# One tile and one product for k and q of the gated delta heads, q without its meta columns, and a new list of places for the steps of the mix

## What is computed

```python
h = concatenate([meta, x])                          # 272 tokens
p = rms_norm(h) @ w_in                              # k, v, q, z of the delta branch; q, k, v of the other (fox)
q, k, v = silu(causal_conv(p_q, p_k, p_v))          # 4 taps
q, k = l2_normalize(q) * DK ** -0.5, l2_normalize(k)
a_mat = strict(k_beta @ k.T * decay)                # k by k
w_val, w_key = triangular_solve(a_mat + I, ...)
qk_intra = causal(q @ k.T * decay)                  # k by q
o, S = scan over chunks of (qk_intra, q * exp(g), k, w_val, w_key)
h = h + (sigmoid(gate_a) * (y_a @ w_o_gdn) + sigmoid(gate_b) * (y_b @ w_o_fox)) @ w_out
```

## Time and profile before

| | |
|---|---|
| median of 3 runs | 2969.7 us (2968.08 to 2970.41) |
| profiled execution | 2970.13 us, its span 2968.4 us |
| TensorE busy | 2916.4 us, 98% of the span |
| DVE, ACT busy | 1926.5 us (65%), 1450.7 us (49%) |
| mean granted TensorE clock | 0.989 |
| DMA | 159 GB/s over the span |

### The profile page before, as it was taken

How to read it: one execution, slowest core, us unless ns; L and a number is a source line. 1 busy time by engine, 2 the same in 40 slices (tenths; PEclk the granted TensorE clock), 3 DMA queues, 4 the chain that set the end, 5 groups by cost and what they waited for, 6 DMA issues and landing times.

```text
span 2968.4 us, 56482 instructions
## 1 busy us (share of the span) xinstructions
PE 2916.4 (98%) x20507; PEld 2677.9 (90%) x20507; DVE 1926.5 (65%) x3349; ACT 1450.7 (49%) x2515; POOL 277.0 (9%) x229
## 2 busy tenths in 40 slices
PE   7999999999999999999999999999999999999998
PEld 7999999999999799998888888888899998999987
DVE  6667776777677454445775665656776666767766
ACT  5555655565556444444444443444545444445543
POOL 0000000000000000001550000000450002400014
PEclk9999999999999899999999999999999999999999
DMA  5434343434343255555555555555554444543344
GB/s 192 143 120 141 120 147 120 138 123 144 122 134 127 93 184 184 188 179 196 181 184 190 183 191 177 190 192 183 190 181 168 143 160 145 179 163 132 133 138 173
DMA packets 128959, 472.94 MB, mean 159 GB/s; under 512 B 14368, under 2 KB 14368, under 8 KB 128672
## 3 DMA queue, kind: packets, MB, share of 16 engines
q1 hardware_dynamic: 126144, 459.46, 46.1%
q0 software_dynamic: 2656, 11.33, 1.2%
HBM read 468.50 MB, written 2.24 MB: 159 GB/s over the span
## 4 chain that ended last, share of the span: by engine, by line
PE 94%; POOL 2%; issue 2%; DVE 1%; ACT 1%; DMA 1%; POOLq 0%; DVEq 0%; ACTq 0%
PE bank L286 20%; PE bank L288 17%; PE bank L289 16%; PE bank L290 16%; PE bank L287 10%; PE bank L725 1%; PE bank L797 1%; PE bank L776 1%; PE bank L958 1%; PE bank L793 1%; POOL late_sum L432 1%; POOL late_sq L428 1%; PE bank L952 1%; PE bank L1030 1%; PE bank L1029 1%
## 5 line engine op out<-in xcount | busy, mean ns | idle before, releaser
L262 DVE TENSOR_TENSOR w_lo<-raw,w_hi 128x1024 fp32r<-128x1024 f32 x866 | 1063.0, 1253 | 249.7 <-ACT w_hi L256 240.5
L256 ACT ACTIVATE w_hi<-raw 128x1024 fp32r<-128x1024 f32 x866 | 898.1, 1053 | 419.5 <-PE bank L287 339.6
L288 PE MATMUL bank<-u,w_hi 128*128 128x256 f32 (+1 forms) x3328 | 1007.8, 303 | 11.7 <-DVE w_lo L262 6.8
L289 PE MATMUL bank<-u,w_hi 128*128 128x256 f32 (+1 forms) x3328 | 950.1, 285 | 0.0
L290 PE MATMUL bank<-u,w_lo 128*128 128x256 f32 (+1 forms) x3328 | 948.4, 285 | 0.0
L288 PEld LDWEIGHTS bank<-u,w_hi 128*128 128x128 f32 x3328 | 631.1, 190 | 36.5 <-issue 22.1
L289 PEld LDWEIGHTS bank<-u,w_hi 128*128 128x128 f32 x3328 | 630.5, 189 | 3.7
L290 PEld LDWEIGHTS bank<-u,w_lo 128*128 128x128 f32 x3328 | 630.2, 189 | 0.0
L286 PE MATMUL bank<-ya,w_hi 128*128 128x512 f32 x1536 | 541.8, 398 | 0.0
L287 PE MATMUL bank<-ya,w_lo 128*128 128x256 f32 x1536 | 430.5, 280 | 0.0
L286 PE MATMUL bank<-u,w_hi 128*128 128x512 f32 x1024 | 359.4, 395 | 0.0
(11 more groups left out here) (365 smaller groups left out, 3757.4 us busy)
## 6 DMA issues: line engine op xcount, KB each, us to landing
raw<-in_stream SPq DMA_DIRECT2D x868, 512.0 KB, 3.4
mix_row<-rows POOLq DMA_DIRECT2D x16, 408.0 KB, 3.9
xT<-in_xT SPq DMA_DIRECT2D x4, 544.0 KB, 6.1
h<-in_xT POOLq DMA_DIRECT2D x1, 2048.0 KB, 9.6
out_dram<-h SPq DMA_DIRECT2D x4, 512.0 KB, 2.6
consts<-in_consts POOLq DMA_DIRECT2D x1, 1921.0 KB, 9.4
vecs<-in_vecs POOLq DMA_DIRECT2D x1, 166.5 KB, 7.0
consts<-in_consts POOLq DMA_DIRECT2D x1, 137.0 KB, 5.9
```

Source lines behind the costliest of these rows:

```text
L256: act.activation(w_hi[:, slot], raw[:, slot], ACT.Copy).then_inc(hi_ready, 1)
L262: dve.tensor_tensor(w_lo[:, slot], raw[:, slot], w_hi[:, slot].bitcast(F32), ALU.subtract).then_inc(lo_ready, 1)
L288: pe.matmul(o, a, x[:, 0], start=first, stop=False)
L289: pe.matmul(o, a, x[:, 1], start=False, stop=False)
```

## The change

- k and q share a tile `kq` of two halves. One product per chunk, with k's chunk as weights and both halves as 256 columns, gives k by k and k by q side by side in bank 6. The meta part of k by k stays in bank 5. The step `qk` of TensorE is gone; `kk` now waits for `unit q` too, and for bank 6 (`gdn y` of the head before). `b mat` and DVE's `qk` read bank 6; `b mat` has one small instruction more.
- q's projection has 260 columns instead of 272 (four meta columns stay for the taps), and conv, tanh, silu, square, sum, root and unit of q have 256 instead of 272.
- The three lists have new places and, in part, another order.

```diff
+Q_FROM = META - 4
+        def u_q(k):
+            return u[:, k, :, Q_FROM:]
-        kT, vT, qT = (mt(x, [P, TOK]) for x in ("kT", "vT", "qT"))
+        kq, vT = mt("kq", [P, 2, TOK]), mt("vT", [P, TOK])
+        kT, qT = kq[:, 0], kq[:, 1]
         PE_PLAN = (
-            (28, "columns"), (76, "k sum"), (81, "turn"), (87, "kk"), (94, "q sum"), (98, "transpose"), (100, "qk"),
-            (105, "prod", 1), (106, "fq sum"), (109, "step", 1), (110, "fk sum"), (111, "prod", 2), (118, "logits"),
-            (120, "step", 2), (120, "turn v"), (120, "prod", 3), (123, "step", 3), (123, "turn p"), (123, "prod", 4),
-            (125, "step", 4), (128, "fox out"), (128, "prod", 5), (131, "meta v"), (132, "step", 5), (135, "prod", 6),
-            (140, "meta state"), (141, "step", 6), (143, "k state", 0), (147, "v new", 0), (152, "state", 0),
-            (167, "k state", 1), (169, "v new", 1), (171, "state", 1), (179, "o sum"))
+            (30, "columns"), (77, "k sum"), (82, "turn"), (85, "q sum"), (93, "kk"), (98, "fq sum"),
+            (100, "transpose"), (106, "prod", 1), (109, "step", 1), (109, "fk sum"), (113, "prod", 2),
+            (117, "logits"), (119, "step", 2), (119, "turn v"), (119, "prod", 3), (122, "step", 3), (122, "turn p"),
+            (122, "prod", 4), (124, "step", 4), (126, "prod", 5), (130, "fox out"), (133, "meta v"), (134, "step", 5),
+            (138, "prod", 6), (140, "meta state"), (141, "step", 6), (143, "k state", 0), (149, "v new", 0),
+            (155, "state", 0), (160, "k state", 1), (164, "v new", 1), (168, "state", 1), (179, "o sum"))
         ACT_PLAN = (
-            (29, "columns"), (56, "tanh", "v"), (64, "tanh", "q"), (65, "tanh", "k"), (67, "tanh", "z"),
-            (69, "k square"), (69, "k root"), (78, "cols"), (80, "decay"), (82, "q square"), (87, "turned"),
-            (93, "q root"), (101, "fq square"), (105, "fq root"), (105, "fk square"), (111, "fk root"), (114, "soft"),
-            (126, "f v"), (127, "f pt"), (127, "f out"), (140, "v new m"), (142, "state"), (152, "v new", 0),
-            (169, "v new", 1), (175, "o square"), (179, "o root"), (182, "y hi"))
+            (25, "columns"), (57, "tanh", "v"), (64, "tanh", "q"), (65, "tanh", "k"), (67, "tanh", "z"),
+            (69, "k square"), (69, "k root"), (80, "q square"), (80, "cols"), (87, "decay"), (87, "q root"),
+            (91, "fq square"), (93, "turned"), (104, "fq root"), (109, "fk square"), (109, "fk root"), (113, "soft"),
+            (125, "f v"), (126, "f pt"), (126, "f out"), (139, "v new m"), (139, "state"), (151, "v new", 0),
+            (169, "v new", 1), (175, "o square"), (179, "o root"), (184, "y hi"))
         DVE_PLAN = (
-            (40, "conv", "v"), (49, "conv", "q"), (54, "silu", "v"), (59, "conv", "k"), (62, "silu", "q"),
-            (63, "silu", "k"), (70, "unit k"), (72, "g diff"), (72, "fox bias"), (78, "silu", "z"), (85, "decay b"),
-            (86, "b mat"), (90, "unit q"), (92, "qk"), (94, "q dec"), (96, "level", 0), (98, "mask", 1),
-            (110, "unit fq"), (111, "level", 1), (111, "unit fk"), (113, "mask", 2), (114, "logits"),
-            (114, "level", 2), (118, "mask", 3), (120, "soft"), (121, "level", 3), (123, "mask", 4),
-            (127, "level", 4), (127, "f out"), (127, "mask", 5), (128, "level", 5), (129, "final"), (135, "mask", 6),
-            (137, "level", 6), (146, "rhs", 0), (156, "state"), (167, "rhs", 1), (180, "y"), (182, "y lo"))
+            (50, "conv", "v"), (55, "conv", "q"), (55, "silu", "v"), (60, "conv", "k"), (61, "silu", "q"),
+            (63, "silu", "k"), (70, "unit k"), (72, "g diff"), (72, "fox bias"), (79, "silu", "z"), (82, "decay b"),
+            (85, "unit q"), (89, "qk"), (94, "b mat"), (94, "level", 0), (95, "q dec"), (97, "mask", 1),
+            (107, "level", 1), (109, "unit fq"), (110, "unit fk"), (111, "mask", 2), (113, "logits"),
+            (113, "level", 2), (116, "soft"), (119, "mask", 3), (123, "level", 3), (123, "mask", 4),
+            (126, "level", 4), (126, "f out"), (126, "mask", 5), (126, "level", 5), (128, "final"), (128, "mask", 6),
+            (133, "level", 6), (148, "rhs", 0), (159, "state"), (163, "rhs", 1), (179, "y"), (189, "y lo"))
             def pe_kk(n):
                 pe.wait_ge(sem("unit k"), n)
+                pe.wait_ge(sem("unit q"), n)
                 if n > 1:
                     pe.wait_ge(sem("prod"), 6 * (n - 1))
-                for t0, w in MAIN_FIRST:
-                    mm = pe.matmul(bank[5][0:w, t0:t0 + w], kT[:, t0:t0 + w], kT[:, t0:t0 + w], start=True,
-                                   stop=True)
-                mm.then_inc(sem("kk"), 1)
+                    pe.wait_ge(sem("gdn y"), 2 * (n - 1))
+                for c, (t0, w) in enumerate(MAIN):
+                    pe.matmul(bank[6][:, c * SEQ:(c + 1) * SEQ].rearrange("p (s n) -> p s n", s=2), kT[:, t0:t0 + w],
+                              kq[:, :, t0:t0 + w], start=True, stop=True)
+                pe.matmul(bank[5][0:META, 0:META], kT[:, 0:META], kT[:, 0:META], start=True,
+                          stop=True).then_inc(sem("kk"), 1)
-            def pe_qk(n):
...
+                    if j == ORDER["q"]:
+                        x, w = u_q, TOK - Q_FROM
...
-                dve.tensor_tensor(b_mat[:], bank[5][:, 0:FOLD], decay_b[:], ALU.mult).then_inc(sem("b mat"), 1)
-                dve.scalar_tensor_tensor(out=prod[:, META:], in0=bank[5][:, FOLD:TOK], scalar=col[:, 2, 0:1],
+                dve.tensor_tensor(b_mat[:, META:], bank[6][:, 0:P], decay_b[:, META:], ALU.mult).then_inc(sem("b mat"), 1)
+                dve.tensor_tensor(b_mat[:, 0:META], bank[5][:, 0:META], decay_b[:, 0:META], ALU.mult).then_inc(
+                    sem("b mat"), 1)
+                dve.scalar_tensor_tensor(out=prod[:, META:], in0=bank[6][:, SEQ:SEQ + P], scalar=col[:, 2, 0:1],
                                          in1=decay_t[:], op0=ALU.mult, op1=ALU.mult).then_inc(sem("b mat"), 1)
```

More of the change, by code:

```diff
@@ L750, in pe_turn @@
                 mm.then_inc(sem("v turned"), 1)
-            def pe_qk(n):
-                pe.wait_ge(sem("unit q"), n)
-                if n > 1:
-                    pe.wait_ge(sem("gdn y"), 2 * (n - 1))
-                for t0, w in MAIN:
-                    mm = pe.matmul(bank[6][0:w, t0:t0 + w], kT[:, t0:t0 + w], qT[:, t0:t0 + w], start=True,
-                                   stop=True)
-                mm.then_inc(sem("qk"), 1)
             def pe_transpose(n):
@@ L894, in _ @@
             steps_pe = {"k sum": lambda n: ones_sum("gdn k", n, TOK), "kk": pe_kk, "turn": pe_turn, "columns": pe_columns,
-                        "q sum": lambda n: ones_sum("gdn q", n, TOK), "qk": pe_qk, "transpose": pe_transpose,
+                        "q sum": lambda n: ones_sum("gdn q", n, SEQ), "transpose": pe_transpose,
                         "fq sum": lambda n: ones_sum("fox q", n, SEQ), "fk sum": lambda n: ones_sum("fox k", n, TOK),
@@ L1187, in act_tanh @@
                     y = {"v": vT, "q": qT, "k": kT}[x]
-                    act.activation(gate_th[:], y[:], ACT.Tanh, scale=0.5).then_inc(sem("silu tanh"), 1)
+                    first = META if x == "q" else 0
+                    act.activation(gate_th[:, first:], y[:, first:], ACT.Tanh, scale=0.5).then_inc(sem("silu tanh"), 1)
             def act_k_square(n):
@@ L1198, in act_q_square @@
                 act.wait_ge(sem("length rs"), norm_of_head("gdn k", n))
-                square("gdn q", n, qT[:], TOK, 0.5)
+                square("gdn q", n, qT[:, META:], SEQ, 0.5)
             def act_fq_square(n):
@@ L1241, in act_decay @@
                     act.wait_ge(sem("decay beta"), n - 1)
-                    act.wait_ge(sem("b mat"), 4 * (n - 1))
+                    act.wait_ge(sem("b mat"), 5 * (n - 1))
                 for c, (t0, w) in enumerate(CHUNKS):
@@ L1313, in _ @@
                          "q square": act_q_square,
-                         "q root": lambda n: root("gdn q", n, TOK, 1.0, ("unit k", n)),
+                         "q root": lambda n: root("gdn q", n, SEQ, 1.0, ("unit k", n)),
                          "turned": act_turned, "fq square": act_fq_square,
@@ L1325, in _ @@
                          "fq": ("fox s", 1), "fk": ("fox s", 1), "fv": ("fox v turned", 1)}
-            dest = {"k": conv_in[0][:, 3:], "v": conv_in[1][:, 3:], "q": conv_in[2][:, 3:], "z": z_raw[:],
+            dest = {"k": conv_in[0][:, 3:], "v": conv_in[1][:, 3:], "q": conv_in[2][:, 3 + Q_FROM:], "z": z_raw[:],
                     "fq": fq[:], "fk": fk[:], "fv": fv[:]}
@@ L1632, in dve_conv @@
                     elif x == "q":
-                        dve.wait_ge(sem("qk"), n - 1)
+                        dve.wait_ge(sem("kk"), n - 1)
                     else:
                         dve.wait_ge(sem("k state"), 2 * (n - 1))
+                first = META if x == "q" else 0
                 for tap in (3, 2, 1, 0):
```

(19 more changed lines are left out.)

6 lines of the change are left out of this document (3 added, 3 removed).

## The result

The changed kernel takes 2978.66 us (median of 9 executions, 2976.56 to 2980.07); the kernel before took 2969.7 beside it (9 executions, 2967.84 to 2973.97). The ratio is 1.0028 with a 95% interval of [1.0019, 1.0038]: slower by 0.28%. The interval excludes no change, and all but its lower end lies beyond 0.2%. 2979.3 us were forecast.

The account below looks back on a forecast made before the run. TensorE was taken as the bound, the mix's time being the sum of its instructions. Savings -4.7, kk's wait +9.8, k sum's wait +3.0 and 17th window +1.5 gave +9.6 us on 2969.7: 2979.3 us, range 2966 to 2987.

Parts of the forecast that it names:

- kk's wait: On TensorE at kk, which now needs unit q: a wait of 0.63 us a head, 9.8 us in all.
- Rivals 1 and 2: First: places on time, only columns show, 2966.5 us, chance 0.18. Second: kk waits 0.3 us, k sum none, some 2972, 0.12.
- Rival 3: Late kk makes b mat late for transpose or prod for DVE: 0.6 us more a head, 2989 us, chance 0.12.
- k sum for k square: TensorE's k sum waits for k square, delayed by DVE's moved conv v: 0.2 us a head, 3.0 us in all.
- the `w_lo` after state starts 0.6 later: On DVE, state starts some 0.9 us later, `w_lo` loses its 0.29 wait, so starts 0.6 us later.
- v new for rhs: In the mix, the rhs was to keep its distance within two places; priced at nothing.
- Columns: q's projection on TensorE: 768 matmuls with 12 columns less, about 5 ns each, save 3.9 us.
- q sum: On TensorE, 16 columns less in two fp32 passes a head save 0.4 us in all.
- Merged product: In kk on TensorE: four passes fewer save 28 ns a head, 0.4 us in all.
- Transpose and the others: Transpose stands 7 places behind kk instead of 11, covered by 0.6 us; it and other moved places priced at nothing.
- 17th window: The window without blocks: soft ahead of mask 3, prod 5 ahead of fox out, together +1.5 us, bounds 0 and +3.

Follow-up runs that it names:

- At 95: The changed kernel with kk at place 95 instead of 93, nothing else; 2968.49 us, ratio to the kernel before 0.9998.

## Why the prediction was right, step by step

**kk's wait: right.** 0.63 us a head forecast, 0.62 measured in head 8, 0.625 as the median of 16 heads, 0.31 in head 1 (0.3 forecast); added up, 10.1 us where 9.8 were forecast (one head near the end of the stage has 0.90). The sum of ACT's rows between k root and q root was 5.85 and is 5.84. That ACT's queue sets it is shown by runs of three kinds (later places, q root first, y hi away). Rivals 1 and 2 needed ACT to close up; it did not. Rival 3 needed the lateness to be passed on; transpose and prod kept their distance, and it ended at kk.

**After a wait: missed.** The passes of a late kk take 0.07 us longer (1.10 against 1.03), 1.1 us in 16 heads. I had counted the wait alone.

**k sum for k square: wrong in size.** 3.0 us were priced, about 0.8 came (k sum's first pass is followed 0.055 us later than before, in 15 heads), and the view of the waits has no row for it. The DVE chain was as written: in the kernel after, the `w_lo` behind state starts at 474.21, conv v at 475.35, conv q at 477.49 and conv k at 480.81, so 3.28 and 3.32 us from one to the next where the sum had 3.30 and 3.33. The step that failed is "the `w_lo` after state starts 0.6 later". Measured against k sum's place it started 0.2 us less late than that. k square was then written at 487.44, which TensorE sees 0.08 us later by the prediction's own handover, at 487.52, and k sum's place came at 487.52:

```profile
487.01 0.43 ACT L1161 ACTIVATE mix_sq<-mix_kq 128x272 f32<-128x272 f32 x1
```

The step was just in time, without margin, where I had computed a deficit of 0.2, and the 0.055 us are what such an arrival costs.

**v new for rhs: missed.** It has no entry in the sum, it costs 1.06 us in 14 windows (1.2 in all), and it goes when conv v goes back ahead of state. But then state is late by as much, so conv v's place decides only which of the two pays. The prediction had put the rhs under "keep their distances".

**Columns: undersized, then partly lost.** 3.9 forecast, 4.8 with the old lists, inside the bounds. The forecast took the difference of two mean durations (289 and 283 ns); the starts in the same trace of before follow at 125.4 and 117.9 ns, which is 7.5 ns for 16 columns, 5.6 for twelve, where 5 were taken and 6.3 came. In the new lists all matmuls at 256 and 260 columns follow 0.8 ns later, and 1.8 us of it are lost again. I saw nothing in the trace of before that pointed to this. q sum was 0.4 in the sum and 0.7 measured.

**Merged product: right.** 0.4 forecast, 0.4 measured beside two products in the same step. In the changed kernel the 1.1 us behind the wait outweigh it.

**Transpose and the others: right at 93.** The 0.6 us cover was there. At 95 it was gone, as 2 x 0.38 of it went to kk, and transpose cost 0.09 us a head.

**17th window: wrong in size.** +1.5 priced, +0.4 measured from end to end. The two effects of order are there in the run that undoes them, 0.47 us and up to 1.46. What I did not price is that the clock level moves with them: in the kernel after it fell 2.6 us later behind the last block than in the kernel before, which can have offset part of the new order's cost. At the same late course of the clock the new order takes 2 us more, inside the bounds and above the 1.5.

**The sum.** -4.7 + 9.8 + 3.0 + 1.5 = +9.6 was forecast and +9.0 measured (medians), and part of that closeness is chance. For the 16 windows the measured terms are kk's wait 10.1, passes behind it 1.1, v new 1.2, k sum 0.8, slower distance 1.8, columns and q sum -5.5, merged product -0.4: together +9.1, where the windows show +7.7. The other 1.4 us were gained in places that I priced at nothing (turn p with prod 4, for one, has 25.75 us in 14 windows instead of 26.70). The forecast had +8.1 for the same windows. It had k sum too high by 2.2 and the columns with q sum too low by 1.2; the terms that it lacked (passes behind the wait, v new, slower distance, less the 1.4) come to +2.7 and nearly cancel these. That is luck. The 1.0 us behind the mix cannot be laid to the change: no step there differs, and in the twelve profiled executions that part takes anything from 1955.0 to 1960.3 us. kk's wait alone decided the sign. The rule of the Trainium skill ("Perfetto Trace Analysis", section "Identifying Performance Opportunities") that a gain comes from the most-contended engine holds for the kernel with q narrowed alone, where the relief shows in full. It does not for the change, where TensorE had less to do and waited.

**Open.** Why matmuls of 256 and 260 columns follow 0.8 ns later with the new lists, but for conv v's part in fq's tile, and which course the clock takes in the 17th window with one and the same list.

## What to carry to other kernels

Where one engine is full and its steps have places in a list, merging two steps gives the merged step the later of two due times. Before that, sum up the rows of the in-order queue that makes the later input, from a common event to both engines: here 7.44 us on TensorE against 8.07 on ACT and DVE gave the loss to 0.01 us a head, and one number in a list was worth 10 us, more than all that the change could save.

Try the parts alone. The column saving on the old lists was worth 0.2% by its windows, and it was the new places around it, kk's above all, and not its own cost, that turned it into a loss of 0.3%.

## What the hardware showed that was not expected

- A pass that starts after a wait is followed later: the fp32 passes of kk take 1.10 us behind a wait of 0.27 or of 0.62 us, and 1.03 without one. A step can be at this verge without a wait in the view of waits; the mean of its group rises by 25 to 38 ns (v new 298 instead of 273, transpose 305 to 311 instead of 273).
- In the mean, matmuls of 260 columns follow at 119.1 ns, those of 256 at 117.9 and those of 272 at 125.4, so the first 4 columns over 256 cost 1.2 ns and the next 12 cost 6.3.
- TensorE's clock fell to half in the 17th window after 5 us in some profiled executions and after 14 us in others, with 7.4 to 8.3 us of matmul time in the ten-microsecond stretches up to and with the fall in both. Where it fell late it also came back sooner (13.7 and 17.1 us at half instead of 27.3 and 30.7). With the new order that is 2.7 to 3.8 us of the window, with the old one 4.3 to 4.8.
